# Weight-quarter sums of a down projection as 32 slice transfers, paced by the slots of the second up projection

## The reference

```
first block :  x += g1 * rms(pool_mixer(modulate(rms(x))));  x += g2 * rms(conv_ffn(...))
second block:  for i in 0, 1:
    h = rmsnorm(x);  m = fox_mixer(h) if i == 0 else s5_mixer(h)
    x = x + rmsnorm(m)
    h = rmsnorm(x)
    x = x + rmsnorm((silu(h @ w_gate) * (h @ w_up)) @ w_down)      # 1024 -> 2816 -> 1024
```

## Time and profile before

| what | value |
|---|---|
| median of 3 runs | 1725.66 us (1725.29 to 1725.81) |
| the profiled execution, its own time | 1728.59 us |
| its span | 1726.8 us |
| TensorE busy | 1639.1 us (95%) |
| granted TensorE clock, mean over the span | 0.979 |
| DMA moved | 242.29 MB, 140 GB/s in the mean |

### The profile page before, as it was taken

One profiled execution on the slowest core, in us unless ns is written; L12 is line 12 of the kernel. 1 busy time (PEld: TensorE's weight loads), 2 busy tenths in 40 slices (PEclk: granted clock), 3 DMA queues, 4 the chain that ended last, 5 costly groups with the idle time before them and its releaser, 6 DMA issues.

```text
span 1726.8 us, 21684 instructions
## 1 busy us (share of the span) xinstructions
PE 1639.1 (95%) x8385; PEld 1357.2 (79%) x8385; DVE 1019.2 (59%) x1645; ACT 679.0 (39%) x1078; POOL 247.0 (14%) x753
## 2 busy tenths in 40 slices
PE   6499999999999999968999999999989999999998
PEld 5388888888877778747888888888878888888886
DVE  6988666677546677625333336666736633333676
ACT  4454333313436767624222222234224522222454
POOL 2011600000027777710000000000010000000000
PEclk8799999999999999979999999999999999999999
DMA  8922222334432222199942234558973232222564
GB/s 350 374 76 97 97 98 98 122 106 132 126 100 71 71 80 71 56 263 253 253 139 96 97 98 126 147 161 231 250 170 124 86 109 98 98 98 98 158 190 146
DMA packets 150136, 242.29 MB, mean 140 GB/s; under 512 B 29217, under 2 KB 112529, under 8 KB 146706
## 3 DMA queue, kind: packets, MB, share of 16 engines
q1 hardware_dynamic: 130898, 210.49, 37.8%
q0 software_dynamic: 4224, 23.07, 5.4%
q10 hardware_dynamic: 14912, 7.34, 1.7%
HBM read 223.05 MB, written 40.89 MB: 153 GB/s over the span
## 4 chain that ended last, share of the span: by engine, by line
PE 85%; DVE 6%; DMA 5%; ACT 2%; issue 1%; POOL 0%; ACTq 0%; POOLq 0%; SPq 0%; DVEq 0%; PEldq 0%
PE bank L2014 26%; PE bank L2015 26%; PE bank L2016 26%; DVE ada L1338 2%; DMA raw<-in_fox_out 1%; PE bank L2328 1%; PE bank L2301 1%; PE bank L2146 1%; DMA u_scratch<-us 1%; PE bank L2457 1%; DMA yfm<-y_scratch 1%; DVE w_lo L1235 1%; PE bank L2054 1%; DMA raw<-in_up 1%; DVE htok L1322 1%
## 5 line engine op out<-in xcount | busy, mean ns | idle before, releaser
L2014 PE MATMUL bank<-hh,w_hi 128*128 128x512 f32 (+1 forms) x1440 | 552.9, 384 | 10.2 <-POOL hl L2009 6.0
L2016 PE MATMUL bank<-hh,w_lo 128*128 128x512 f32 (+1 forms) x1440 | 549.1, 381 | 0.0
L2015 PE MATMUL bank<-hl,w_hi 128*128 128x512 f32 (+1 forms) x1440 | 549.1, 381 | 0.0
L1235 DVE TENSOR_TENSOR w_lo<-raw,w_hi 128x1024 fp32r<-128x1024 f32 (+1 forms) x282 | 335.8, 1208 | 203.2 <-ACT w_hi L806 199.2
L806 ACT ACTIVATE w_hi<-raw 128x1024 fp32r<-128x1024 f32 (+1 forms) x282 | 293.5, 1045 | 388.9 <-DMA raw<-in_dn 116.8
L2014 PEld LDWEIGHTS bank<-hh,w_hi 128*128 128x128 f32 x1440 | 272.7, 189 | 64.2 <-POOL hl L2009 6.9
L2016 PEld LDWEIGHTS bank<-hh,w_lo 128*128 128x128 f32 x1440 | 272.6, 189 | 52.1
L2015 PEld LDWEIGHTS bank<-hl,w_hi 128*128 128x128 f32 x1440 | 272.9, 190 | 50.1
L2014 PE MATMUL bank<-w_hi,hid 128*128 128x512 f32 x352 | 138.2, 392 | 0.0
L2016 PE MATMUL bank<-w_hi,hid 128*128 128x512 f32 x352 | 137.1, 389 | 0.0
L2015 PE MATMUL bank<-w_lo,hid 128*128 128x512 f32 x352 | 137.0, 389 | 0.0
(11 more groups left out here) (324 smaller groups left out, 2171.3 us busy)
## 6 DMA issues: line engine op xcount, KB each, us to landing
raw<-in_up SPq DMA_DIRECT2D x132, 512.0 KB, 3.2
raw<-in_dn SPq DMA_DIRECT2D x55, 512.0 KB, 4.1
ada<-in_ada_w SPq DMA_DIRECT2D x24, 1024.0 KB, 8.4
v_scratch<-in_dn POOLq DMA_DIRECT2D x6, 2816.0 KB, 21.7
raw<-in_fox_in SPq DMA_DIRECT2D x32, 512.0 KB, 3.3
raw<-in_s_w SPq DMA_DIRECT2D x24, 512.0 KB, 4.1
raw<-v_scratch SPq DMA_DIRECT2D x20, 512.0 KB, 3.7
v_scratch<-v_scratch POOLq DMA_DIRECT2D x2, 2816.0 KB, 12.9
```

The costliest lines, as they stand in the source:

```text
L1235: dve.tensor_tensor(w_lo[:, n % RING, 0:w], raw[:, n % RING, 0:w], w_hi[:, n % RING, 0:w].bitcast(F32), ALU.subtract).then_inc(lo_done, 1)
L2014: pe.matmul(dst, w_h, r_h, start=first, stop=False, skip_group_check=True)
L2015: pe.matmul(dst, w_h, r_l, start=False, stop=False, skip_group_check=True)
L2016: return pe.matmul(dst, w_l, r_h, start=False, stop=last, skip_group_check=True)
```

## The change

GpSimd's eight quarter transfers become 32 slice transfers of 128 x 1408 numbers (704 KB): each of the eight steps is done as four slices m = 0 to 3. Each transfer waits for all transfers before it (the first for none), and transfer t also waits until `slot_mm` has reached S_UP2 + 2 + t + 1, so that there is at most one new transfer for each slot of the second up projection. The place in GpSimd's program stays the same. SP's wait counts 32 transfers instead of eight.

```diff
-            sp.wait_ge(v_step, 16 * 8)
+            sp.wait_ge(v_step, 16 * 32)
...
-            def rows_of(quarter):
-                return quarter.rearrange("m p c -> (m p) c")
-
-            quarter = dram["dn3"].rearrange("(q m) p c -> q m p c", q=4)
-            steps = ((0, quarter[0], False), (2, quarter[1], False), (0, quarter[1], True), (2, quarter[3], True),
-                     (1, v_dram[0], False), (1, quarter[3], True), (3, v_dram[1], False), (3, quarter[2], True))
-            for t, (to, src, add) in enumerate(steps):
-                if t >= 2:
-                    pool.wait_ge(v_step, 16 * t)
-                if add:
-                    pool.dma_start(rows_of(v_dram[to]), rows_of(src), max_dma_last_dim=4 * FH * P, accum_op=ALU.add)\
-                        .then_inc(v_step, 16)
-                else:
-                    pool.dma_start(rows_of(v_dram[to]), rows_of(src), max_dma_last_dim=4 * FH * P).then_inc(v_step, 16)
+            def weight_sums(start):
+                quarter = dram["dn3"].rearrange("(q m) p c -> q m p c", q=4)
+                steps = ((0, quarter[0], False), (2, quarter[1], False), (0, quarter[1], True), (2, quarter[3], True),
+                         (1, v_dram[0], False), (1, quarter[3], True), (3, v_dram[1], False), (3, quarter[2], True))
+                for t, ((to, src, add), m) in enumerate(itertools.product(steps, range(4))):
+                    pool.wait_ge(slot_mm, start + t + 1)
+                    if t:
+                        pool.wait_ge(v_step, 16 * t)
+                    if add:
+                        pool.dma_start(v_dram[to, m], src[m], max_dma_last_dim=4 * FH * P, accum_op=ALU.add)\
+                            .then_inc(v_step, 16)
+                    else:
+                        pool.dma_start(v_dram[to, m], src[m], max_dma_last_dim=4 * FH * P).then_inc(v_step, 16)
+            weight_sums(S_UP2 + 2)
```

## The result

The changed kernel takes 1699.05 us (median of 4 runs, 1697.34 to 1701.21) against 1725.47 us for the kernel before on the same chip (4 runs, 1721.93 to 1725.81). The ratio is 0.9852, 95% interval 0.9834 to 0.987. The profiled execution took 1701.21 us with a span of 1699.4 us. The forecast was 1700.4 us within 1697 to 1709.

What follows compares the result with a forecast made beforehand. TensorE is 85% of the chain, so only its stalls or lower clock give time: differences of 18.62, 5.73 and 1.50 make 25.85 us, less 0.5 for margin 25.3; 1725.66 − 25.3 = 1700.4 us, range 1697 to 1709.

Steps and rivals of the forecast that it cites:

- The stall and its owner: Fox output tail to third up slot: TensorE waits 21.0 us for late loads beside GpSimd's weight sums, which the change moves away.
- The gain in the place: Fox output tail to third up slot: 25.85 us over the clean path, less 0.5 us, gives 25.3 us.
- The anchor of the tail: Start of the Fox output tail, taken as 748.60; from there to the first transposes 30.86 us against 12.24, difference 18.62.
- the twin: Output tail of S5 (q = 4): same 96 matmuls, transposes and up opening without weight sums, taken as the clean path's price.
- The split between waiting and the lower clock: Of the 25.85 us in tail and up opening, 21.0 us waits and about 4.9 us matmuls at the lower clock.
- What is late next: Fox output tail: the kernel's own sixth, seventh and eighth slot loads would all be in time, the last by 1.1 us.
- the margin: Eighth Fox output slot: split at 751.6, wanted at 752.7, so 1.1 us; 0.5 us of gain kept back for it.
- The chain: 32 slice transfers beside the second up projection: copies 5.44 us, adds 6.7, 194 us in all, from 792.0 to near 986.
- The cover of the up loads: Second up projection: loads issued 21.8 us ahead of need cover slower landings beside the sums; priced at nothing, at most 4.5 us.
- Rival 1: Tail or up projection: another wait takes over part of the stall; gain 17 us, 1708.7 us; chance 8%.
- Rival 2: Fox output tail: loads were late for their own sake and the sums innocent; gain near 0, 1725.7 us; chance 2%.
- Rival 3: GpSimd: the 32 transfers delay `hl` and TensorE's gate products; 1764 us at 16 us a step, extreme 2861; together 3%.

Runs made afterwards that it cites:

- experiment 1: Kernel before with its eight whole-quarter transfers, only the first now waiting for slot_mm >= S_UP2 + 3; 1699.61 us, ratio 0.9842.
- experiment 3: Changed kernel without any weight sums or SP's wait for them, the last products loading plain quarters of dn3; 1699.68 us, ratio 0.9839.
- experiment 8: Changed kernel with the sums as 128 serial transfers of 32 rows, only the first waiting for a slot; 1790.13 us, ratio 1.0392.
- experiment 9: Changed kernel with the sums as 256 serial transfers of 16 rows, only the first waiting for a slot; 2085.46 us, ratio 1.2103.
- experiment 5: Kernel before with the two opening copies left in place and the six other transfers held until slot_mm >= S_UP2 + 3; 1719.29 us, ratio 0.9972.
- experiment 6: Kernel before with all eight transfers held until slot_mm >= S_FO + 2, when SP issues the seventh Fox output slot; 1718.73 us, ratio 0.9954.
- experiment 7: Kernel before with all eight transfers held until slot_mm >= S_FO + 3, when SP issues the eighth Fox output slot; 1710.10 us, ratio 0.9889.
- experiment 4: Kernel before with the second opening copy also waiting for the first, so one quarter is in flight instead of two; 1725.66 us, ratio 0.9993.

## Why the prediction was right

**The stall and its owner** were as forecast, by experiments 1 and 3. The gain in the place was 26.47 us, forecast 25.3, and the total 26.4 us by the medians.

**The anchor of the tail was one slot off.** The prediction let the tail begin at 748.60, right at the gap. From 779.46 back, the twin's 54 matmuls do not fit behind the first gap: only 48 stand there, six before and 42 after the second gap. The first tail slot had been in the ring, so the tail began at 748.60 − 6 × 0.227 = 747.24, and its first part cost 32.22 − 12.24 = 19.98 us over the twin instead of 18.62. That makes the sum 27.21 us. Of it 0.74 us stayed: 0.45 in the tail up to 761.99 and 0.29 up to 779.63. The split between waiting and the lower clock, forecast as 21.0 and 4.9 us, was 20.8 and 5.7 us.

**What is late next** was right in kind. The sixth and seventh slot landed in 3.4 and 6.9 us, in time. The eighth was priced with the 4.2 us of a quiet stretch and took 5.9 us; when it was issued, the second gain row, the seventh slot and the turn store were still under way. It was ready at 745.40 + 5.9 + 2.3 = 753.6 and wanted at 753.4. That the margin came out within 1.3 us of the 1.1 forecast is luck: the landing was 1.7 us too short and, by the anchor, the need 1.4 us too late, while the issue at 745.11 was itself 1.8 us later than on the clean path, where SP is not held by the turn store (743.34, that is 745.40 less the 2.06 us by which this execution runs later). The three errors nearly cancel. The 0.5 us kept for the margin is close to the 0.45 us that stayed in the tail.

**The chain** ran from 793.93 to 996.34 and landed near 1003; forecast 986, bounds 966 and 1023. From issue to issue an add took 7.4 us in the mean where 6.7 was forecast, in the upper part of the 5.4 to 8.0, so the fixed part does not vanish. A copy took 5.7, not the 5.44 of a slot: it was mostly paced by the one before it and not by the slot. With the start 1.9 us later these make the 17 us. In all the 32 slices took 66 us longer than the eight quarters of experiment 1 (some 209 us against 143), where the prediction gave an estimate of 48.

**The cover of the up loads** held: 4.0 us in the median and 6.3 at most up to 880, and no wait for `w_lo`. Experiment 1 shows that it also holds for whole quarters.

**Rival 1** did not come. **Rival 2** is refuted by experiment 3. **Rival 3**, the chain that blocks GpSimd, is real as a mechanism (experiments 8 and 9), but its point of decision was put too late: 14.0 us a step was computed for the second pair of `hl`, and with 1223 it is an estimated (1223 − 792) / 32 = 13.5 us. The slices at 6.5 us are far from it.

**What the prediction missed** is the other side of the sum: the time of the kernel before. It took the stall of one profile as a constant. The stall depends on whether GpSimd issues the copies before or after SP's slot loads (experiments 5 to 7), and the time at which GpSimd is ready for them differs by 6 us between two executions of one program. Beside experiment 5 the kernel before lay between 1714.70 and 1728.66 us. The gain of the changed kernel against its median was 22.8 us there and 26.4 us in the first comparison; the kernels of experiments 1 and 3, which have no stall either, gained 27.9 us beside their own. The forecast took the stall of one profile from the median of other executions, so that the total came out within 1.4 us of it is in part luck. The changed kernel starts its sums by a count of slots, and its eight runs stayed within 4 us. That part of the spread of the kernel before is the order of issue is likely but not shown, since no execution of it with the other order was profiled; the one run of 1699.69 us in experiment 7, with the order set by hand, stays unexplained too.

## What to carry to other kernels

A bulk transfer that nothing needs for a long time should be tied to a point of the consumer's progress where the ring has its full lead, not left to start when its engine happens to be free: here the place gave all of the gain, and cutting the transfers up gave nothing more. When two queues meet, look which one issues first, since here a load issued 0.3 us ahead of the bulk landed in 6.9 and 8.8 us, and those issued behind it in 13 to 24. And count what stands behind a serial chain on its own engine: more and smaller transfers lengthen it (6.5 us a step for 704 KB, still 3.2 us for 88 KB), until the engine's next work is late.

## What the runs showed of the hardware

Two 2816 KB copies on GpSimd's queue, issued 0.3 us behind a 512 KB load on SP's queue, left that load at 6.9 us; the next load, 2.4 us behind the copies, took 18.4 us (experiment 6). With the copies 0.3 us behind the eighth slot, that load took 8.8 us, where it took 5.9 in the changed kernel (experiment 7). Whether one or two copies were in flight made no difference to the total (experiment 4).

The size of a transfer pays less and less: slices of 704, 176 and 88 KB took 6.53, 4.10 and 3.20 us a step, with the adds in the mix. An eighth of the bytes costs half of the time.

Behind the copies the issuing queue itself can be held up. In the kernel before, SP's issue of the first up slot took 10.80 us, where issues of this kind take 0.3 to 0.4 us in the changed kernel (timeline of SP's queue, 737 to 760):

```profile
750.00 10.80 SPq L571 DMA_DIRECT2D raw<-in_up  x1
```

In experiment 4 the same issue took 3.72 us and the turn store's 4.17 us. In experiment 6, with the copies issued only behind the seventh slot, it took 0.34 us although they were in flight. So transfers in flight do not hold up an issue by themselves; what does is open.

TensorE's clock followed its stops: 0.67 granted in 748.6 to 779.5 before, where it was busy half of the time, 1.00 in the same window after. Of the 26.5 us gained, 5.7 were matmuls that ran at the lower clock and 20.8 were waits.
